# Moving helper work between the projections and the attention units of a two-block network on one core

## What is computed

```python
# block 1, per layer (first_block)
z = modulate(rmsnorm(x)) @ w_in            # q, k, v, u, g
attn = softmax(q k^T) v                    # 8 query heads, 2 kv heads, keys = 256 ctx + 512 latent
gm = gelu(u) * (w_spatial @ layernorm(gelu(g)) + b)
x = x + ga1 * (concat(attn, gm) @ w_out);  x = x + ga2 * (relu(h @ w_ff1)^2 @ w_ff2)
# block 2, per layer (second_block)
x = x + 0.5 * swiglu(...)
z = rmsnorm(x) @ w_in                      # q_a 256, kv_a 128, k_rope 32, pool 256, fox qkv 3*384, fox gate 6
ya = mla_mixer(...)    # 6 heads: q from rmsnorm(q_a) @ w_q_b, k and v from rmsnorm(kv_a) @ w_kv_b, rope on 32
yb = pool_mixer(...)   # windowed means, a 64x64 product per group, a scale
yc = fox_mixer(...)    # 6 heads with a decay row c = cumsum(log_sigmoid(gate))
x = x + concat(ya, yb, yc) @ w_out;  x = x + 0.5 * swiglu(...)
```

## Time and profile before

| what | value |
|---|---|
| median of 3 runs | 3560.59 us (3558.07 to 3560.93) |
| profiled execution, own time | 3562.94 us |
| its span, first to last instruction | 3561.2 us |
| instructions | 47213 |
| granted PE clock, mean over the span | 0.979 of full speed |

### The profile page before, as it was taken

One profiled execution on the slowest core, in us unless ns is written; L12 is line 12 of the kernel. 1 busy time (PEld: TensorE's weight loads), 2 busy tenths in 40 slices (PEclk: granted clock), 3 DMA queues, 4 the chain that ended last, 5 costly groups with the idle time before them and its releaser, 6 DMA issues.

```text
span 3561.2 us, 47213 instructions
## 1 busy us (share of the span) xinstructions
PE 3422.3 (96%) x17172; PEld 2808.7 (79%) x17172; DVE 1832.8 (51%) x2785; ACT 1203.1 (34%) x1886; POOL 364.7 (10%) x415
## 2 busy tenths in 40 slices
PE   8989999999998999999999889999999998799999
PEld 5867888888877788888888567888788886678887
DVE  6766866455457444454345645434543456554343
ACT  4454222122156332233232354323332323543232
POOL 0013200000202200020002123000200021230001
PEclk9979999999998999999999989999999999999999
DMA  6300343333220133333334112333333332123332
GB/s 224 115 24 25 96 135 112 118 119 129 65 71 14 54 100 95 97 92 101 93 96 111 52 31 60 101 93 96 93 99 95 95 101 64 30 60 95 95 99 89
DMA packets 551252, 314.76 MB, mean 88 GB/s; under 512 B 31102, under 2 KB 524888, under 8 KB 551128
## 3 DMA queue, kind: packets, MB, share of 16 engines
q1 hardware_dynamic: 550608, 312.99, 29.5%
q10 hardware_dynamic: 520, 0.13, 0.0%
HBM read 310.98 MB, written 2.10 MB: 88 GB/s over the span
## 4 chain that ended last, share of the span: by engine, by line
PE 86%; DVE 7%; ACT 4%; issue 2%; POOL 1%; DMA 0%; SPq 0%; DVEq 0%; ACTq 0%; POOLq 0%
PE ps L874 25%; PE ps L876 24%; PE ps L878 24%; PE ps L1428 2%; PE ps L1461 2%; DVE nmax L2415 1%; ACT w_hi_sb L1495 1%; PE ps L1107 1%; DVE scr L2144 1%; DVE scr_r L1975 1%; PE ps L969 1%; PE ps L968 1%; PE ps L970 1%; PE ps L1394 1%; ACT scr L1865 1%
## 5 line engine op out<-in xcount | busy, mean ns | idle before, releaser
L1909 DVE TENSOR_TENSOR w_lo_sb<-w_raw,w_hi_sb 128x1024 fp32r<-128x1024 f32 (+1 forms) x460 | 587.7, 1278 | 1236.7 <-ACT w_hi_sb L1495 1234.7
L1495 ACT ACTIVATE w_hi_sb<-w_raw 128x1024 fp32r<-128x1024 f32 (+1 forms) x460 | 506.3, 1101 | 1337.1 <-PE ps L878 1300.8
L874 PE MATMUL ps<-hh_lat,w_lo_sb 128*128 128x512 f32 x1712 | 682.2, 399 | 19.7 <-DVE z L2011 8.0
L876 PE MATMUL ps<-hl_lat,w_hi_sb 128*128 128x512 f32 x1712 | 670.9, 392 | 0.0
L878 PE MATMUL ps<-hh_lat,w_hi_sb 128*128 128x512 f32 x1712 | 669.3, 391 | 0.0
L874 PEld LDWEIGHTS ps<-hh_lat,w_lo_sb 128*128 128x128 f32 x1712 | 323.3, 189 | 93.6 <-issue 19.7
L876 PEld LDWEIGHTS ps<-hl_lat,w_hi_sb 128*128 128x128 f32 x1712 | 323.6, 189 | 68.2 <-issue 4.9
L878 PEld LDWEIGHTS ps<-hh_lat,w_hi_sb 128*128 128x128 f32 x1712 | 322.7, 189 | 66.7
L874 PE MATMUL ps<-h2h,w_lo_sb 128*128 128x512 f32 x704 | 275.1, 391 | 1.9 <-DVE z L2384 1.5
L874 PE MATMUL ps<-m2h,w_lo_sb 128*128 128x512 f32 x704 | 273.9, 389 | 0.0
L878 PE MATMUL ps<-h2h,w_hi_sb 128*128 128x512 f32 x704 | 273.9, 389 | 0.0
(11 more groups left out here) (386 smaller groups left out, 5490.4 us busy)
## 6 DMA issues: line engine op xcount, KB each, us to landing
w_raw<-in_ffn_w_gu SPq DMA_DIRECT2D x176, 512.0 KB, 3.8
w_raw<-in_w_ff SPq DMA_DIRECT2D x128, 512.0 KB, 4.0
w_raw<-in_ffn_w_down SPq DMA_DIRECT2D x64, 704.0 KB, 4.5
z<-in_w_mod SPq DMA_DIRECT2D x64, 512.0 KB, 5.1
w_raw<-in_w_in SPq DMA_DIRECT2D x56, 512.0 KB, 3.9
w_raw<-in_w_out SPq DMA_DIRECT2D x32, 512.0 KB, 3.8
scr<-in_w_mod SPq DMA_DIRECT2D x16, 512.0 KB, 5.1
scr<-in_w_mod SPq DMA_DIRECT2D x2, 2048.0 KB, 14.7
```

The costliest lines, as they stand in the source:

```text
L874: mm = nc.tensor.matmul(dst, wl, hi[:, k, 0:n], start=(k == 0), stop=False)
L876: mm = nc.tensor.matmul(dst, wh, lo[:, k, 0:n], start=False, stop=False)
L1495: nc.scalar.activation(w_hi_sb[:, slot, 0:width], w_raw[:, slot, 0:width], ACT.Copy).then_inc(S["w_hi"], 1)
L1909: nc.vector.tensor_tensor(w_lo_sb[:, slot, 0:width], w_raw[:, slot, 0:width], w_hi_sb[:, slot, 0:width].bitcast(F32), ALU.subtract).then_i ...
```

## The change

It changes no arithmetic. It changes in which unit or on which side of a split and a take some instructions stand.

- `low_behind`: DVE's low halves of a head (`prepare`, `prepare2`) come 2 units (nq = 4) or 1 unit (nq = 2) after ACT's high halves, in place of the same unit. `lower_out` comes as much later after `take_out`. The gated tiles' low halves go from even units from 4 to odd units from 5. `lower_k` is cut into two halves at units 4 and 6 in place of both at unit 2.
- `prepares`: in block 2, pairs 2 and up have ACT's high halves at steps 1 and 3 of the pair in place of 3 and 5 (so DVE's low halves stay at 3 and 5; those of pairs 0 and 1 go to 5 and 7).
- Beside block 2's units: query 4 from unit 3 to 4 on PE (its take on ACT and DVE from 4 to 5), query 5 from 5 to 7 (take from 6 to 8), keys of pair 2 from 7 to 9 (ACT's copies from 8 to 10), pooling products from 9 and 11 to 13 and 16 (DVE's scale from 10 and 12 to 14 and 17), value transposes from 13, 15, 17 to 19, 22, 25 (ACT's copies from 14, 16, 18 to 20, 23, 26). DVE's low half of a weight split comes two units after ACT's high half.
- In the ten steps ahead of the attention: ACT's split goes from the head of a step to its end; on DVE the helpers stand first, then the take, then the split. So each step's helpers no longer stand behind the wait for chunk c. The second square root goes from step 3 to 4, the first reciprocal from 3 to 4, the second from 4 to 5, the rotated key part from 5 to 4; the gate's exponential and logarithm go from ACT's step 8 to 9, behind the copy of query 2.

```diff
-            at = ((1, 3) if st.nq > 2 else (0, 2)) if st.first else (3, 5)
+            at = ((1, 3) if st.nq > 2 else (0, 2)) if st.first or pair > 1 else (3, 5)
...
+        def low_behind(st):
+
+            return 2 if st.nq > 2 else 1
...
# PE, beside_units
-                    if u == 3:
+                    if u == 4:
                         pe.wait_ge(S["mla_kc"], mx.at("mla_kc", 8))
                         mla_query(mx, 4)
-                    if u in (5, 7):
+                    if u in (7, 9):
...
-                    if u in (9, 11):
+                    if u in (13, 16):
...
-                    if u in (13, 15, 17):
+                    if u in (19, 22, 25):
...
# ACT, the ten steps of linear_z2
-                            split(st.chunk0 + c + 2, c % 2, KD, z2_width(st, c + 2))
                             if 1 <= c <= 3:
                                 act.wait_ge(S["z_taken"], st.at("z_taken", c))
                                 nc.scalar.activation(mla_sq[c - 1], zt(Z2_TILES[c - 1]), ACT.Square).then_inc(S["mla_sq"], 1)
...
+                            if c in (3, 4):
+                                act.wait_ge(S["mla_ms"], mx.at("mla_ms", c - 2))
+                                root(mla_rs[4 - c], bank(8 - c)).then_inc(S["mla_root"], 1)
...
+                            split(st.chunk0 + c + 2, c % 2, KD, z2_width(st, c + 2))
# DVE, the ten steps
                         for c in range(Z2_AHEAD):
-                            split(st.chunk0 + c + 2, c % 2, KD, z2_width(st, c + 2))
-                            take_z2(st, c)
...
+                            take_z2(st, c)
+                            split(st.chunk0 + c + 2, c % 2, KD, z2_width(st, c + 2))
...
# DVE, beside_units and the attention loop
-                    c = next_split(u)
+                    c = next_split(u - 2)
...
-                            if st.first and u >= 4 and u % 2 == 0 and u // 2 - 1 <= len(st.gm):
+                            if st.first and u >= 5 and u % 2 and u // 2 - 1 <= len(st.gm):
...
-                            if u < U and prepares(st, u):
+                            w = u - low_behind(st)
+                            if 0 <= w < U and prepares(st, w):
...
-                            if st.first and st.last_keys and u == 2:
-                                lower_k(st.qk, 1)
-                            v = u - lag(st) - 3
+                            if st.first and st.last_keys and u in (4, 6):
+                                lower_k(st.qk, 1, (u // 2 - 2,))
+                            v = u - lag(st) - 3 - low_behind(st)
```

More of the change, by code:

```diff
@@ L669, in next_split @@
         def next_split(u):
+            if u < 0:
+                return None
             c = 16 if u == S_WIDE - 1 else chunk_ends(u) and chunk_ends(u) + 1
@@ L1039, in beside_units @@
                             mla_keys(mx, 2)
-                    if u in (9, 11):
-                        j = (u - 9) // 2
+                    if u in (13, 16):
+                        j = (u - 13) // 3
                         if j == 0:
@@ L1709, in _ @@
                                 prepare2(mx, 1)
+                            if c == 9:
+                                query_copy(mx, 2)
                                 act.wait_ge(S["fox_a"], mx.at("fox_a", 1))
@@ L2034, in beside_units @@
                                                      ).then_inc(S["fox_c"], 1)
[L2035 to L2038, removed]
+                    if u in (5, 8):
+                        rope_query(mx, 4 + (u - 5) // 3)
+                    if u in (14, 17):
+                        j = (u - 14) // 3
                         dve.wait_ge(S["pool_y"], mx.at("pool_y", j + 1))
@@ L2045, in beside_units, with lower_k @@
                             low(hl_lat[:, 3 + j, :], zt(3 + j), hh_lat[:, 3 + j, :]).then_inc(S["pool_lo"], 1)
-                    c = next_split(u)
+                    c = next_split(u - 2)
                     if c is not None:
                         split(st.z2.chunk0 + c, c % 2, KD, z2_width(st.z2, c))
-                def lower_k(qk, kv):
+                def lower_k(qk, kv, halves=(0, 1)):
                     own = slice(64 * kv, 64 * kv + 64)
                     dve.wait_ge(S["k_his"], qk.at("k_his", 2 * kv + 2))
-                    for half in range(2):
+                    for half in halves:
                         low(k_lo[kv][64 * half:64 * half + 64, :], k_all[own, :], k_hi[own, kv, :]
@@ L2266, in _ @@
                         for c in range(Z2_AHEAD):
[L2267 to L2269 removed]
+                            if c == 4:
                                 dve.wait_ge(S["mla_root"], mx.at("mla_root", 2))
                                 link(nc.vector.reciprocal(mla_rs[0], mla_rs[0]))
[L2272 to L2274 removed]
+                            if c == 5:
                                 link(nc.vector.reciprocal(mla_rs[1], mla_rs[1]))
[L2276 removed]
                                 normed(2, R_KVA + st.l, mla_rs[1])
[L2279 to L2283 removed]
                             if c == 6:
@@ L2297, in _ @@
                                 prepare2(mx, mx.at("q_his", 3), 1)
+                            take_z2(st, c)
+                            split(st.chunk0 + c + 2, c % 2, KD, z2_width(st, c + 2))
+                            if c == 4:
+                                for k in range(2):
+                                    normed(k, R_QA + 2 * st.l + k, mla_rs[0])
+                                dve.wait_ge(S["rope_loaded"], 32)
+                                x = zt(14)[64:96, :]
+                                link(nc.vector.tensor_tensor(mla_tb[64:96, :], zt(14)[96:128, :], rope[96:128, 1, :], ALU.mult))
+                                link(nc.vector.tensor_tensor(x, x, rope[64:96, 0, :], ALU.mult))
+                                nc.vector.tensor_tensor(x, x, mla_tb[64:96, :], ALU.add).then_inc(S["mla_kr"], 1)
                             if c == 9:
```

35 lines of the change are left out of this document (13 added, 22 removed).

## The result

The changed kernel takes **3462.47 us** (median of 4 runs, 3461.85 to 3462.9) where the kernel before takes 3560.07 (3558.07 to 3560.93): a ratio of 0.9726, interval 0.971 to 0.9743. The gain is 97.6 us. I had forecast 49 and a range that ended at 3480, so the sign was right and the size was half of what came.

The account below looks back on a forecast made before the run. Outside the PE-bound feed-forward products, the order of instructions waiting for one another was the bound. Terms 12.7 + 10 + 7 + 3 + 3 + 15 = 50.7, plus 3 (clock), less 4 (replacement waits), gave 50: 3511 us, range 3480 to 3542.

Parts of the forecast that it names:

- A: Block 2's ten steps: splits at the step's end remove PE's waits for value copies and mean square, 12.7 us.
- B and D: Block 2's units: later helpers in units 0 to 9 gain 10 us, later value transposes 3 us.
- I take half, 2.8: Take at unit 6 of block 2: half of its 5.4 us of PE's wait gained.
- C and E: Block 2's units: takes at units 12 and 24 gain 7 us, scores waiting at L1409 gain 3.
- F: Block 1: later low halves end DVE's 25.7 us of waits for query heads' high halves, 15 us gained.
- I take 0.75 for each: Block 1: 0.75 us gained for each of DVE's 20 waits for high halves, 15 us.
- E's third of L1409: Block 2's scores: a third of PE's waits at L1409 (6.3 for exponentials, 3.2 for the unit-30 take) gained, 3 us.
- The clock: Whole kernel: fewer products at 1.2 GHz after long waits, 3 us gained beyond the waits themselves.
- Half is taken up: Attention units: the chain of exponentials, copies and row maxima replaces PE's removed waits, 3530 us; chance 0.22.
- More: Whole change: every wait counted is gained in full, block 1's heads at 25 us, 3485 us; chance 0.13.
- Slower: Ten steps: splits behind helpers come after their use and PE waits every step, over 2.9 us each; chance 0.07.
- Low halves beside POOL: Heads' and keys' 44 low halves beside POOL's normalising cost DVE 26 us, 3537 us; part of a 0.22 chance.

Follow-up runs that it names:

- e6: Kernel before with only block 2's heads moved: high halves earlier for pairs 2 and up, low halves and outputs two units behind; 3522.55 us, ratio 0.9888.
- e7: Kernel before with only the low halves of block 1's query heads and of finished outputs later; 3534.96 us, ratio 0.993.
- e5: Kernel before with only the helpers and leftovers of block 2's units moved, with the later DVE split; 3554.79 us, ratio 0.9982.
- e4: Changed kernel with a 1.95 us DVE delay once in block 1 (unit 12) and once in block 2 (unit 30); 3463.47 us.
- e8: Changed kernel with 1.95 us DVE delays ahead of each of units 12 to 15 in block 1's first latent attention and block 2's first layer; 3475.16 us.
- e15: Changed kernel with 12 useless products on PE ahead of part 0 of unit 6, the wait for the take left in place; 3459.03 us.
- e11: Kernel before with three more unread products per unit on PE, in the context attention and block 2's units 33 to 39; 3559.76 us, ratio 0.9993.
- e10: Changed kernel with query 4's rotation on DVE at unit 6, behind the take, in place of unit 5; 3454.47 us, ratio to before 0.97.

## Why the prediction was wrong

- **A, 12.7 forecast, 17.0 measured alone.** The mechanism was right, and all of it ACT's. PE's idle time fell by 5.8 us a layer (6.7 to 0.94), 11.5 in all; what was missing are 2.1 us a layer by which the products got faster (66.20 to 64.06 busy, clock 0.98 to 1.00). The late splits behind helpers cost nothing that can be measured, as I said.
- **B and D, 13 forecast, 7.2 measured alone, about 10 on top of e6** (49.7 less 39.4). "I take half, 2.8" for the take at unit 6 was wrong: the two takes there cost PE 6.1 us in the changed kernel and 5.4 before, and DVE's queue is as I described it, a low half and a rotation ahead of the take. I had the right queue and gave it a gain. Query 4 gave more than its 3.0 (L1007's wait went from 5.8 to 0.4 us), and the pooling product and the transposes no longer wait, as forecast.
- **C and E, 10 forecast, 39.4 measured.** This is the step that failed most: I priced block 2's low halves by PE's waits alone (8 at L2011, a third of those at L1409), where the waits that count are DVE's own for the high halves. In F, I had looked at those. The same list of the kernel before has this for block 2, 39.0 us in 24 times:

```profile
DVE scr_r L1975 <- ACT scr_r L1520: 12.6, 10, 1.3
DVE scr_r L1975 <- ACT hl_ctx L1520: 8.8, 4, 2.8
DVE scr_r L1975 <- ACT hh_ctx L1520: 8.4, 4, 3.0
DVE hl_ctx L1975 <- ACT hl_ctx L1520: 4.8, 4, 1.3
...
DVE hh_ctx L1975 <- ACT hh_ctx L1520: 4.4, 2, 2.2
```

(The expectation of e6 gives them as 34.6 in 26; it missed the last line and miscounted.) In e6 all five are gone, and `hl_lat` lost 6.6 more (54.1 to 47.5, the finished outputs): 45.6 us of waits removed, 39.4 us gained.

- **F, 15 forecast, 27.0 for the heads and 29.4 for all of block 1.** "I take 0.75 for each" of 20 waits was too low: they are 25.7 us, 1.28 each. And the outputs' low halves, which the same edit moves, I left out: in e7 `hl_lat` lost 7.5 us and `hl_ctx` 3.6. That makes 36.8 us of waits removed and 27.0 gained. I had measured the excess of a pair with a wait, 2.3 us, correctly (in e7 the same units, 9 to 11, last 2.3 us less), and then cut it down because DVE still idles in an undisturbed pair. That idle time was no sign that a chain would take over: DVE waits there for PE's scores, which I read as one chain in which PE, DVE and ACT follow one another.
- **Units 32 to 47, nothing forecast, 16.5 measured** (a part of the 39.4 and 10 above). Only E's third of L1409 touched them. They waited 6.7 us a layer in 7 turns for ACT's copies and ran at 0.84. The heads' halves alone give 5.1 of the 8.3 us of layer 0 (e6), the helpers alone 0.2 (e5), the rest comes with both.
- **The clock, 3 forecast.** The products are faster by 36.6 us. In the sum 50.7 less 4 stood for waits; PE's idle time fell by 63.5. How much of the 36.6 is a gain of its own, and how much only fills with products what was idle time, stays open over the whole kernel: at unit 6 the half clock costs up to 2.7 us a layer and once nothing (e4, e8, e15), and in the sparse stretches of e11 a higher clock with fillers shortened nothing.
- **Rivals.** *Half is taken up* was wrong: no other chain took the place. *More* had the direction, at 3485, but in block 2 counted PE's waits only. *Slower* did not happen. *Low halves beside POOL* happened, and its price was right for those it hit: 6 of DVE's 16 `q_hl` subtractions of 512 columns, which start 0.26 us behind a POOL normalising, took 1.18 to 1.20 us, the other ten 0.69. But in block 2 POOL paid in DVE's place: of its 24 normalisings of 128 x 512, six that start behind a subtraction with both operands in SBUF took 1.57 to 1.59 us, the other 18 0.69 to 0.70, also the eight beside a subtraction that reads `ps` (PSUM). In these cases whoever started first kept its time. DVE's busy time rose by 6.0 us and POOL's by 22.9, not DVE's by 26, and PE's waits for POOL went from 2.2 to 1.6 us: on POOL there was room. The Trainium skill (GPSIMD Engine Reference, Specifications) says that GpSimd shares its SBUF interfaces with VectorE and contends with DVE instructions that have two SBUF inputs; the trace agrees, in both directions.

DVE and POOL in the changed kernel, in order of time: POOL first, DVE first, and DVE reading `ps`:

```profile
236.51 0.91 POOL L2512 TENSOR_SCALAR scr<-scr,rinv 128x768 f32<-128x768 f32 x1 [0.34 <-DVE rinv L2429]
236.77 1.18 DVE L1979 TENSOR_TENSOR q_hl<-z,q_hl 64x512 fp32r<-64x512 f32 x1
...
2002.85 1.27 DVE L1979 TENSOR_TENSOR scr_r<-scr,hl_ctx 96x512 fp32r<-96x512 f32 x2
...
2003.03 1.57 POOL L2512 TENSOR_SCALAR scr<-scr,rinv 128x512 f32<-128x512 f32 x1 [3.55 <-DVE rinv L2429]
...
2047.13 0.67 DVE L1979 TENSOR_TENSOR scr_r<-ps,scr_r 128x512 fp32r<-128x512 f32 x1
2047.30 0.69 POOL L2512 TENSOR_SCALAR x_ctx<-x_ctx,rinv 128x512 f32<-128x512 f32 x1 [1.06 <-DVE rinv L2429]
```

The corrected sum goes by kernels that ran: ten steps 17.0, block 1's heads 27.0, its gated tiles and second key 2.4 (29.4 less 27.0), block 2's heads 39.4, its helpers 10.3 on top: 96.1 of 97.6.

## What to carry to other kernels

Where two engines hand each unit of a loop back and forth, an extra instruction of the second that waits for the first in the same unit costs most of its wait, in every unit that has one, even when PE's list names other lines and both engines are half idle: price it by the waiting engine's own list (here 73 and 86 of 100 parts of such waits came back), and put one unit between producer and consumer. Each group of such waits has to be priced by the same method in every stage, those behind the last changed instruction too. A hole ahead of a stretch in which PE has a full load can cost the half clock behind it on top of its length (here 0 to 2.7 us for a hole of 3.05): move what holds up the take (e10, 8.0 us); useless products in the hole are worth a try where it must stay.

## What the runs showed of the hardware beyond that

A single idle stretch of 2 us left the granted clock at 1.00 (e4), four with little work between them brought it to 0.83 over 20 us (e8), and 3 us at unit 6, in a stretch that was sparse before it, was followed by products at 1.2 GHz (0.43 us apart in place of 0.23) in five of six cases and at 2.4 GHz in one. With twelve products into an unread bank in its place, 2.99 us, they came at 2.4 GHz in both layers of e15. By the Trainium skill (TensorE: Matmul & The Clock Gate, What's actually happening) activity releases the array to the higher clock. The runs agree: in e11 three more products per unit took it from 0.66 to 0.91, though the stretch, with them in it, did not get shorter.
